# The sample tokens' retrieval picks placed singly among the last tile's

## The reference, cut to what matters

```
def block(tb):                                    # tokens x 1024, after an RMSNorm
    q = (tb @ w_q).reshape(blk, 8, 2, 128)
    s1 = einsum('thd,hnd->thn', q[:, :, 0], keys1)
    s2 = einsum('thd,hnd->thn', q[:, :, 1], keys2)
    v1, i1 = top_k(s1, 16); v2, i2 = top_k(s2, 16)
    cand = v1[..., :, None] + v2[..., None, :]    # 256 a head
    top_s, top_j = top_k(cand, 16)
    expert = take_along_axis(cand_idx, top_j)     # 8 heads x 16 experts a token
    gate = softmax(top_s)
    pre = einsum('thkd,td->thk', u_tab[expert], tb)
    act = gelu(pre) * gate
    return einsum('thk,thkd->td', act, v_tab[expert])
```

## Time and profile before

| | |
|---|---|
| median of 3 runs | 3511.97 us (3508.84 to 3517.49) |
| the profiled execution | 3530.2 us |
| its span (first to last instruction) | 3528.4 us |
| mean granted TensorE clock | 0.92 |
| TensorE, DVE, ScalarE, POOL busy | 82%, 66%, 34%, 35% of the span |
| bytes moved | 1225 MB, 347 GB/s on average |

### The profile page before, as it was taken

One profiled execution on the slowest core, in us unless ns is written; L12 is line 12 of the kernel. 1 busy time (PEld: TensorE's weight loads), 2 busy tenths in 40 slices (PEclk: granted clock), 3 DMA queues, 4 the chain that ended last, 5 costly groups with the idle time before them and its releaser, 6 DMA issues.

```text
span 3528.4 us, 31686 instructions
## 1 busy us (share of the span) xinstructions
PE 2898.8 (82%) x9764; PEld 1660.0 (47%) x9764; DVE 2340.0 (66%) x5028; ACT 1198.0 (34%) x3519; POOL 1233.6 (35%) x1094
## 2 busy tenths in 40 slices
PE   7889598888988788797987898788878787888775
PEld 6767375555565356354632256355455332222222
DVE  3444787886667897687566596767667777435444
ACT  3211354332333342433233332432323343324333
POOL 0100123554334433444333333343334343424332
PEclk9989798998899899898999899898899899989998
DMA  4205488999999999999999799999899899979996
GB/s 145 78 1 177 185 334 322 347 371 399 374 400 415 375 393 375 381 390 386 411 421 421 293 396 398 360 350 419 362 411 420 346 407 382 418 320 391 421 422 276
DMA packets 183660, 1225.42 MB, mean 347 GB/s; under 512 B 21185, under 2 KB 21585, under 8 KB 48194
## 3 DMA queue, kind: packets, MB, share of 16 engines
q0 software_dynamic: 153088, 1115.26, 78.7%
q1 hardware_dynamic: 30402, 108.14, 8.1%
HBM read 1211.47 MB, written 11.84 MB: 347 GB/s over the span
## 4 chain that ended last, share of the span: by engine, by line
PE 40%; DMA 29%; DVE 18%; ACT 5%; issue 4%; DVEq 2%; POOL 1%; SPq 0%; ACTq 0%; POOLq 0%
PE ps L510 40%; DMA ring<-in_uv,picked 27%; DVE ring L2053 6%; DVE otok L2012 1%; ACT scratch L1012 1%; ACT diag L1012 1%; DVE scratch L1818 1%; DMA wring<-in_weights 1%; DVEq L1855 1%; POOL ring L495 1%; ACT L1012 1%; ACT gated L1012 1%; DMA out_o_gla<-scratch 1%; ACT act_v L1012 1%; DVE scratch L1859 1%
## 5 line engine op out<-in xcount | busy, mean ns | idle before, releaser
L510 PE MATMUL ps<-ring,diag 128*128 128x512 f32 (+1 forms) x3348 | 1727.8, 647 | 404.8 <-ACT diag L1012 399.4
L495 POOL DMA_INDIRECT ring<-in_uv,picked x1024 | 1164.3, 1137 | 1897.8 <-PE ps L510 1350.8
L2053 DVE SCALAR_TENSOR_TENSOR ring<-ring,htok 128x1024 f32<-128x1024 f32 x1024 | 1249.8, 1228 | 663.8 <-DMA ring<-in_uv,picked 658.1
L510 PEld LDWEIGHTS ps<-ring,diag 128*128 128x128 f32 (+1 forms) x3348 | 618.8, 200 | 1267.1 <-ACT diag L1012 729.4
L1012 ACT ACTIVATE act_v<-pre 128x1 f32<-128x1 f32 x1040 | 210.4, 202 | 1772.4 <-DVE ring L2053 1771.6
L510 PE MATMUL ps<-hT,wring 128*128 128x256 f32 (+1 forms) x3200 | 752.7, 391 | 37.9 <-DVE hT L1328 22.8
L510 PEld LDWEIGHTS ps<-hT,wring 128*128 128x128 f32 x3200 | 621.1, 195 | 209.8 <-issue 86.9
L1012 ACT ACTIVATE diag<-masks,gated 128x128 f32<-128x128 f32 x821 | 329.7, 402 | 31.0 <-PE ps L510 4.3
L1012 ACT ACTIVATE gated<-act_v,gates 128x1 f32<-128x1 f32 x1024 | 301.7, 295 | 33.3
L2012 DVE SCALAR_TENSOR_TENSOR otok<-ring,gated,otok 128x1024 f32<-128x1024 f32 x197 | 252.6, 1282 | 0.0
L510 PEld LDWEIGHTS ps<-scratch 128*128 128x128 f32 (+2 forms) x1428 | 196.9, 202 | 106.3 <-issue 65.2
(11 more groups left out here) (308 smaller groups left out, 1549.7 us busy)
## 6 DMA issues: line engine op xcount, KB each, us to landing
wring<-in_weights SPq DMA_DIRECT2D x200, 512.0 KB, 7.8
ring<-in_uv,picked POOLq DMA_INDIRECT x1024, 11.3
scratch<-in_keys POOLq DMA_DIRECT2D x4, 1024.0 KB, 11.4
scratch<-in_s_gla POOLq DMA_DIRECT2D x4, 1024.0 KB, 12.1
out_o_gla<-scratch POOLq DMA_DIRECT2D x4, 1024.0 KB, 11.2
xT<-in_xT SPq DMA_DIRECT2D x1, 2080.0 KB
scratch<-in_s_dn POOLq DMA_DIRECT2D x1, 2048.0 KB, 11.4
scratch<-in_s_ssm POOLq DMA_DIRECT2D x1, 2048.0 KB, 16.6
```

Of the source, the lines that this page charges most:

```text
L495: pool.indirect_dma_start(out=ring[:, g % RING, :], out_offset=None, in_=io["uv"][L], in_offset=bass.IndirectOffsetOnAxis(ap=index, axis=0 ...
L510: return pe.matmul(out, lhsT, rhs, start=start, stop=stop)
L2053: stt(x, x, 1.0, h, MUL, MUL, accum_out=pre[:, g % SMALL:g % SMALL + 1]).then_inc(sem("dotted"), 1)
```

## The change

The sample tokens are no longer units. Their eight picks stand among tile 3's in both layers, each in front of tile 3's pick 72, 79, 86 and so on to 121, so that the running number of all picks still ends at 1039. Their sum has banks 2 and 3 for its own. TensorE issues the spread of a sample pick three picks ahead. ScalarE copies the sample's sum to SBUF (over the sample rows of `htok`, which are no longer needed) three picks after the last sample pick. At the end of tile 3 the 8 small transposes follow the 8 large ones, and one `added` stands for both additions. In layer 1 the order of the choices is turned round as well: tile 3's now has slots from 777 on, 4 steps a slot, and the sample's slots from 820 on.

```diff
-UNITS = [(0, t) for t in (0, 1, 2, 3, S)] + [(1, t) for t in (0, 1, 2, S, 3)]
-SAMPLE = (4, 8)
+UNITS = [(L, t) for L in range(2) for t in range(4)]
+CHOICES = [(L, t) for L in range(2) for t in (0, 1, 2, 3, S)]
+SAMPLE = (4, 9)
+SAMPLE_FROM, SAMPLE_STEP = 72, 7
+def picks(t):
+    order = []
+    for k in range(NPICK):
+        i, rest = divmod(k - SAMPLE_FROM, SAMPLE_STEP)
+        if t == 3 and rest == 0 and 0 <= i < NS_TOK:
+            order.append((S, i))
+        order.append((t, k))
+    return order
+SPREAD_LEAD = 3
 TOPK_AT = [(-1, 1, -1), (0, 4, 127), (211, 5, 255), (256, 5, 383), (290, 6, 511),
-           (438, 2, 519), (521, 5, 647), (739, 6, 775), (777, 6, 903), (793, 3, 911)]
+           (438, 2, 519), (521, 5, 647), (739, 6, 775), (777, 4, 903), (820, 6, 960)]
...
             def spread(L, b):
+                if b == 0:
+                    pe.wait_ge(sem("tail_chosen"), L + 1)
+                    pe.wait_ge(sem("htok_ready"), HTOK[5] if L == 0 else HTOK[9])
+                    pe.wait_ge(sem("root_ready"), norm_no(3, 0) + 1 if L == 0 else norm_no(4, 1) + 1)
                 if b >= 2:
-                    pe.wait_ge(sem("dotted"), FIRST[SAMPLE[L]] + b - 1)
+                    pe.wait_ge(sem("dotted"), SAMPLE_G[L][b - 2] + 1)
...
-                for k in range(COUNT[u]):
-                    g = FIRST[u] + k
-                    if t == S and k + 2 < NS_TOK:
-                        spread(L, k + 2)
+                for j, (t, k) in enumerate(PICKS[u]):
+                    g = FIRST[u] + j
+                    if g + SPREAD_LEAD in SAMPLE_G[L]:
+                        spread(L, SAMPLE_G[L].index(g + SPREAD_LEAD))
...
                             if t == S:
-                                out, weight = ps[0:NS_TOK, h, :], diag[:, d, 0:NS_TOK]
+                                out, weight, n = ps[0:NS_TOK, 2 + h, :], diag[:, d, 0:NS_TOK], NS_TOK
...
+                if unit == 3:
+                    pe.wait_ge(sem("sample_out"), L + 1)
+                    for c in range(KD):
+                        last = pe.transpose(ps[:, 2, c * NS_TOK:(c + 1) * NS_TOK], htok[0:NS_TOK, 2, c * P:(c + 1) * P],
+                                            ident[0:NS_TOK, 0:NS_TOK])
                 last.then_inc(sem("out_mm"), 1)
...
+                    if g == SAMPLE_G[L][-1] + 3:
+                        act.wait_ge(sem("v_done"), TURNED[SAMPLE_G[L][-1] + 1])
+                        f(htok[0:NS_TOK, 2, :].rearrange("p (b i) -> p b i", b=2), ps[0:NS_TOK, 2:4, :], ACT.Copy)\
+                            .then_inc(sem("sample_out"), 1)
...
+                last = tt(x, x, ps[:, 0:2, :].rearrange("p b (c i) -> p (b c) i", c=4), ADD)
+                if t == 3:
+                    x = xT[:, :, TILE_AT[S]:TILE_AT[S] + NS_TOK]
+                    last = tt(x, x, ps[:, 2, 0:KD * NS_TOK].rearrange("p (c b) -> p c b", c=KD), ADD)
+                last.then_inc(sem("added"), 1)
```

More of the change, by code:

```diff
@@ L46 @@
 FIRST_BLOCK = {k: sum(BLOCKS[n] for n, _ in ORDER[:i]) for i, k in enumerate(ORDER)}
-UNITS = [(0, t) for t in (0, 1, 2, 3, S)] + [(1, t) for t in (0, 1, 2, S, 3)]
-SAMPLE = (4, 8)
+UNITS = [(L, t) for L in range(2) for t in range(4)]
[10 more added lines that the diff above has]
+    return order
+PICKS = [picks(t) for _, t in UNITS]
+COUNT = [len(order) for order in PICKS]
+FIRST = [sum(COUNT[:u]) for u in range(len(UNITS) + 1)]
+SAMPLE_G = [[FIRST[4 * L + 3] + PICKS[3].index((S, i)) for i in range(NS_TOK)] for L in range(2)]
 KEPT = ((0, 1, 16), (1, 4, 8), (4, 8, 4), (8, 16, 1))
@@ L56 @@
 NCAND = 64
-COUNT = [NS_TOK if t == S else NPICK for _, t in UNITS]
-FIRST = [sum(COUNT[:u]) for u in range(len(UNITS) + 1)]
-SHARE = {0: "11211111", 1: "11123100", 2: "01221112", 3: "22100000", 5: "01221111", 6: "11222100"}
+SHARE = {0: "11211111", 1: "11123100", 2: "01221112", 3: "22100000", 4: "01221111", 5: "11222100"}
 WHICH = ((), (2,), (1, 3), (1, 2, 3), (0, 1, 2, 3))
-ASIDE = [u in SHARE and 0 < k < COUNT[u] - 1 and k % 4 in WHICH[int(SHARE[u][k // 16])]
-         for u in range(len(UNITS)) for k in range(COUNT[u])]
+ASIDE = [t != S and u in SHARE and 0 < k < NPICK - 1 and k % 4 in WHICH[int(SHARE[u][k // 16])]
+         for u in range(len(UNITS)) for t, k in PICKS[u]]
 SUMMED = [sum(ASIDE[:g]) for g in range(len(ASIDE) + 1)]
@@ L94, in odd_slot @@
 def odd_slot(p, off):
-    return min(ODD_B + off, FIRST[7] - 1) if p else min(ODD_A + off, FIRST[5] - 1)
+    return min(ODD_B + off, FIRST[6] - 1) if p else min(ODD_A + off, FIRST[4] - 1)
 def topk_slot(u, off):
@@ L480, in _ @@
             front.upto(-1)
[L481 to L485, removed]
-                for k in range(COUNT[u]):
-                    g = FIRST[u] + k
+            for u, (L, unit) in enumerate(UNITS):
+                if u:
+                    pool.wait_ge(sem("chosen"), 5 * L + unit + 1)
+                for j, (t, k) in enumerate(PICKS[u]):
+                    g = FIRST[u] + j
                     if u == 0 and k % (GROUP * TOPK) == 0:
                         pool.wait_ge(sem("first_picked"), k // (GROUP * TOPK) + 1)
+                    if t == S:
+                        pool.wait_ge(sem("tail_chosen"), L + 1)
                     index = tail_pick[:, k:k + 1] if t == S else picked[:, HSLOT[t], k:k + 1]
@@ L916, in choice @@
             def choice():
-                for u, (L, t) in enumerate(UNITS):
+                for u, (L, t) in enumerate(CHOICES):
                     rows, p = ROWS[t], t >= 2
@@ L992, in _ @@
                             if t == S:
-                                out, weight = ps[0:NS_TOK, h, :], diag[:, d, 0:NS_TOK]
+                                out, weight, n = ps[0:NS_TOK, 2 + h, :], diag[:, d, 0:NS_TOK], NS_TOK
                             else:
-                                out, weight = ps[:, h, :], diag[:, d, :]
-                            last = mm(out, weight, ring[:, g % RING, D + 512 * h:D + 512 * h + 512], k == 0, k == COUNT[u] - 1)
+                                out, weight, n = ps[:, h, :], diag[:, d, :], NPICK
+                            last = mm(out, weight, ring[:, g % RING, D + 512 * h:D + 512 * h + 512], k == 0, k == n - 1)
                         last.then_inc(sem("v_done"), 1)
-                    if k < COUNT[u] - 1:
+                    if j < COUNT[u] - 1:
                         front.upto(min(g + LEAD, FIRST[u + 1] - 1))
@@ L1840, in topk_step @@
             def topk_step(u, i):
-                L, t = UNITS[u]
+                L, t = CHOICES[u]
                 rows = ROWS[t]
@@ L2033, in _ @@
             choose.upto(-1)
[L2034 to L2043, removed]
+            for u, (L, unit) in enumerate(UNITS):
+                dve.wait_ge(sem("htok_ready"), HTOK[5 * L + unit])
+                for j, (t, k) in enumerate(PICKS[u]):
+                    g = FIRST[u] + j
                     if t == S:
```

50 lines of the change are left out of this document (21 added, 29 removed).

## The result

The changed kernel takes 3481.28 us (median of 5, 3475.62 to 3486.93), the kernel before in the same measurement 3517.49 (3508.84 to 3532.98). The medians differ by 36.2 us. The ratio is 0.9892 with a 95% interval of 0.9865 to 0.9920, which is some 38 us less, between 28 and 47. The two profiled executions (3530.2 and 3475.6 us) lie high and at the very bottom among the runs of their kernels, so their difference of 54.6 us overstates the change, and I read them stretch by stretch.

The account below looks back on a forecast made before the run. Transfers were taken to set the pace, 421 GB/s or 2.5 us a pick, broken where sample tokens are units. 18.6 + 27.0 - 3 - 0.9 = 41.7 us off 3512.0 gave 3470.3, range 3457 to 3488.

Parts of the forecast that it names:

- Layer 0's unit, 18.6: Sample unit taken out of layer 0: layer 1's tile 0 starts 20.3 us earlier, taken as 18.6 for possible clock loss.
- Layer 1's unit, 27.0: Sample unit and its two drains taken out of layer 1: 27.5 us won, 0.5 charged for the remaining stop.
- Single picks, 0: Sample picks put singly in tile 3: each spread's 1.5 us delay is won back over three picks, so 0 us.
- The reserve: Queued gathers in the ring of 7 slots: at most 7.3 us of lateness can vanish, taken as 6.
- The choices moved, a loss of 3: Layer 1's choices: 1.2 us for placing plus 3 for the sample's choice behind it, less 1, net loss 3.
- The tail, a loss of 0.9: At the end, 8 small transposes and the small addition between last pick and final norm lose 0.9 us.
- VectorE's steps holding up gathers, up to 1.6: Denser placing steps with two SBUF inputs could delay gather issue: four of them would be 1.6 us.
- The second, the slower one: Rival: the clock falls in the mixed stretches, at half clock 141 us more, giving 3611; chance 0.03.
- The first: Rival: the reserve doesn't cover spreads or moved choices, giving 3494 or 3477; chance of a 12 to 25 us gain 0.11.
- The rule on waits and the clock: Waits between matmul bursts slow the array: both stops of the new kernel lose the clock, sum 1.7 us less.
- My half for layer 0: Layer 0's remaining stop: clock loss would take 3.4 us back over two picks; half was taken, leaving 18.6.

Follow-up runs that it names:

- sample_860: The changed kernel with the sample tokens' choice for layer 1 at slot 860 instead of 820; 3486.20 us, one execution.
- rate3_860: The changed kernel with layer 1's sample choice at slot 860 and tile 3's choice at 3 steps a pick instead of 4; 3482.54 us, one execution.
- every_second: The changed kernel with the sample picks at every second pick from tile 3's 72nd on (step 1 instead of 7); 3477.12 us.
- spread_thrice: The changed kernel with each of the 16 spreads issued three times, same result; 3514.98 us.
- slow_placing: The changed kernel, choices for layer 1's first tile and tile 3 scanning 4 steps a pick, then placing 1; sample's choice from 836; 3462.55 us.
- cluster_end: The changed kernel with the eight sample picks together behind tile 3's last pick, in their own unit with its drain; 3502.08 us.
- before_again1: The kernel before, unchanged, profiled once more; 3531.73 us, one execution.
- before_again2: The kernel before, unchanged, in a third profiled execution; 3510.70 us, one execution.

## Why the prediction was right

- *Total.* Forecast 41.7 us less and 3470; measured 38 (28 to 47) less and 3481, inside the range of 3457 to 3488. Half of the distance of 11 us is the base: I took the gain off a median of three runs, 3512.0, and the larger sample gives 3517.5. The terms below, read from traces, add up to 47 us with layer 1's mean, 9 more than the 38. The changed kernel's trace is of the fastest of its five executions, and the mixers' part differs by as much: from the first gather to pick 448, where the kernels are the same, ten traces took 1445 to 1457 us. Where the 9 us lie isn't shown.
- *Layer 0's unit, 18.6.* Measured 22.5. The stop is 4.64 us for 4.7 forecast. I had charged 1.7 us for a clock lost in the stop, and it wasn't lost. The other 2.0 are the ten picks in front of it: 6.47 + 15.7 = 22.2 us by my sum, 20.18 in the trace, since I counted 1.98 us for each, and picks in a row take less. The first ran at half clock even so; sample_860 and rate3_860 needed 17.90 us for the same ten.
- *Layer 1's unit, 27.0.* 25.4 against the trace that I had read, by the windows. But across executions it is 16.3 to 29.9, since the clock in the old sample unit differs from one to the next. I had read 0.66 in one execution as a property of the unit. That is the weakest step: it was right for that trace, and the sum over medians should have been smaller. The mean of the three is 23.9. Of the stop that stays I had TensorE 5.3 to 5.5 us late with half clock behind it; it is 3.0 us late at full clock. Nothing of either shows: picks 903 to 976 took 184.7 to 185.6 us in all nine variants of the changed kernel besides it, with the clock lost and without.
- *Single picks, 0.* Right. The stretches took 141.5 and 156.9 us for 140.4 and 158.0, and the lateness is won back in three picks as worked out. The reserve that I took as 6 us is a little smaller: 5.8 us of lateness was hidden in every_second, 6.5 made a hole in spread_thrice.
- *The choices moved, a loss of 3.* Wrong by about 5: by the changed kernel's window they gained 1.5 to 2.1, by those of four more kernels with the same choices up to 3.5. The step that failed was adding 3 us for the sample's choice right behind the placing. At 860 it isn't cheaper than at 820. That placing runs through the reserve was right, and slow_placing took that loss away.
- *The tail, a loss of 0.9.* 0.7: from the start of DVE's last product to the end it is 29.8 us for 29.1.
- *VectorE's steps holding up gathers, up to 1.6.* They do hold them up, and it costs nothing here. An issue takes 0.94 us. Where a product with two SBUF inputs is running as it begins, it takes what is left of the product and 0.8 us more (1.98 us behind the product of 1.23 us at 3293.94). Beside a sample product, whose second input lies in PSUM, it takes 0.94. POOL's busy time in picks 976 to 1039 rose from 59.0 to 69.7 us, by more such meetings, at the same pace:

```profile
3286.62 0.94 POOL L514 DMA_INDIRECT ring<-in_uv,picked  x1 [0.59 <-PE ps L529]
...
3294.01 1.98 POOL L514 DMA_INDIRECT ring<-in_uv,tail_pick  x1 [2.17 <-PE ps L529]
```
- *Rivals.* The second, the slower one, wasn't met, but for a reason that I had only in part. In these runs the clock stayed at 1.00 with two or more picks between two spreads; with one full pick between (cluster_end) or with spreads in a row it fell. The first would have needed spreads that show; doubling them didn't make them show.
- *The rule on waits and the clock* (the Trainium skill, TensorE: Matmul & The Clock Gate, HAM oscillation). As I read it, both stops of the new kernel would have lost the clock; the page speaks of waits between bursts, and each stop here has transposes inside. In the profiled execution neither lost it (1.98 us at 1995.27; five picks in 8.87 us). But that was partly luck. Of ten traces with the changed kernel's stops, layer 1's lost the clock for some 4 us in five, layer 0's was low in one (spread_thrice). In the kernel before, the first stop lost it in both layers in three executions of three. My half for layer 0 rested on the pick at 2020.72, which stands behind the unit's second stop; behind its first, the like of the one that stays, the spread took 3.77 us. The old stops had two spreads in them, the new ones have none, and which of the wait and the spreads cost the clock there isn't shown. The kernel before, then layer 1's stop in every_second:

```profile
1988.47 3.77 PE L510 MATMUL ps<-htok,masks 8*128 8x512 f32 x4 [2.46 <-DVE xT L2029]
```

```profile
3112.60 13.98 PE L529 MATMUL ps<-ring,diag 128*128 128x512 f32 x28 [1.31 <-DVE xT L2048]
```

## What to carry to other kernels

A small item of work that makes one engine slower than the transfers for a few steps costs little when its steps are dealt out, with some distance, among those of a larger one, and twice when it is a phase: once for its own rate, once for the drains around it. Before costing a late engine, measure how far behind it may fall before the queue of transfers runs empty; here that was somewhat under 6 us with seven slots. And spread bursts of a side task over as many steps as it takes to stay below that: this alone was worth about half of what the change was.

## What the runs showed of the hardware

- Matmuls with 8 of 128 rows, twice or three times 1.98 us in a row among full ones, brought the mean granted clock from 1.00 to 0.92 to 0.95 and to 0.86, though TensorE was busier than with one (133 and 156 us for 120 and 136 in the two stretches, with two). With one full pick between two spreads it fell too (3.17 us for a full pick at 3442.45 in cluster_end). In the old sample unit of layer 1, with spreads and 128 x 8 picks in turn, it stayed low for some 7 us of work in one execution and for 29 and 36 in the two others; in layer 0's for 7 to 8 in all three. Each time it came back while the same alternation went on.
- A product on DVE with a PSUM operand (1.22 us) costs what one with two SBUF operands does (1.23), and it leaves the issue of a gather alone: 0.94 us in six meetings of six in layer 1's last stretches, for up to 1.98 beside one with two SBUF operands.
- Executions of one kernel differ by more than 20 us (3508.8 to 3533.0), and most of the difference between two traces (14 us of 21 between before_again1 and before_again2) was the clock in one stretch of 42 to 55 us.
